# A two-layer decoder step on one core: norms and query weights taken ahead, fewer level-two candidates, sample sums as wide rows

## The chip, the cores and the metric

The kernel runs on one core of one Trainium2 chip. The metric is the time of one execution in device microseconds. A lower time is better. All times below are microseconds unless they are marked ns.

## What is computed

One inference step of a decoder trunk with two layers: 512 prompt tokens and 8 sample tokens (520 in all), width 1024, all in 32-bit floats. Layer 0 mixes by mLSTM and RWKV-7, layer 1 by HGRN2. Behind each stands a PEER mixer, which holds most of the time. The reference, cut:

```python
for l in range(DEPTH):                                   # DEPTH = 2
    sh1, sc1, g1, sh2, sc2, g2 = split(silu(c) @ ada_w[l] + ada_b[l], 6)
    h = _rmsnorm(x, norm_mix_g[l]) * (1 + sc1) + sh1
    out = _even_mixer(h, ...) if l % 2 == 0 else _odd_mixer(h, ...)
    x = x + g1 * out
    h = _rmsnorm(x, norm_ffn_g[l]) * (1 + sc2) + sh2
    x = x + g2 * _peer(h, peer_w_q[l], peer_keys[l], peer_u[l], peer_v[l])
y = _rmsnorm(x, norm_final_g)

def _peer(h, w_q, keys, u_tab, v_tab):                   # 8 heads, 2 x 128 keys, 16384 experts
    q = (h @ w_q).reshape(T, 8, 2, 128)
    s = einsum('thcd,hckd->thck', q, keys)
    s_top, i_top = lax.top_k(s, 16)
    cand = s_top[:, :, 0, :, None] + s_top[:, :, 1, None, :]
    best, pos = lax.top_k(cand.reshape(T, 8, 256), 16)   # 16 experts of each head
    gate = jax.nn.softmax(best)
    act = jax.nn.gelu(einsum('thkd,td->thk', u_tab[experts], h))
    return einsum('thk,thkd->td', gate * act, v_tab[experts])
```

## The kernel before

Columns of x and h are tokens, and the 1024 features lie in 8 pieces (DT) of 128 partitions. A product of 32-bit data is made as three matmuls of high and low parts in fp32r (x high by w high, x high by w low, x low by w high): each operand is cast to its high part on ACT, and DVE or POOL subtracts that for the low part. The program is a row of stages, each a block with one instruction list for each engine. An engine enters the next block when all have left the last.

`mix_norm` at the head of a layer squares x on ACT, adds the squares in pairs on DVE, sums over partitions with ones-matmuls (L731), takes root and reciprocal, and scales x. `split_stage` is the projection behind it (L301 with the high parts of the tokens, L309 with the low parts); both output projections (`residual_projection`) use it too, and add the gated result to x on DVE.

`peer_start` (L2266) makes the second norm and the queries: 8 squares (L2391), 8 ones-matmuls (L2351), root (L2396), reciprocal by token halves (L2454), x times it in four steps of 4 pieces (L2463), the high parts of the tokens on ACT (L2402). The query weights come in blocks of 256 columns by DMA (`load_w`, L2284), become high (`high_q`, L2255) and low (`low_q`, L2261) parts, and the first matmuls with them are L2367, those with the low parts of the tokens L2344. The 16 transposes of the keys are L2357.

`peer_hidden` (L2551) goes over all 16384 experts in 128 units. The prompt tokens are handled densely: in a unit PE makes the hidden values of 128 experts for 512 tokens (24 matmuls, L2841), with rows of u that DVE turns (L2224), ACT casts (L2232) and POOL subtracts (L2237). Between these, DVE finds each token's experts (`routing`): for each of the four tiles of 128 tokens it adds 16 by 16 level-one scores to 256 candidates a head (L2667), finds the best 16 of each head by `top16_rows` (MAX L2520 and L2531, FIND_INDEX L2525 and L2536, MATCH_REPLACE L2526), turns positions into two numbers (L2671 to L2675), and picks the keys (L2682 to L2696). PE turns the picks (L2850), behind unit `pick_unit` less LEAD = 2, and then makes the gates in groups of four tokens (the quads, L2868). The generator's `yield` numbers are costs: a planner of the kernel spends 4.4 us of them a unit, and so fixes in which unit each step stands on every engine. For the 8 sample tokens only the chosen rows of u and v are gathered. Their output sums are L2859: for each sample 8 matmuls, each with 128x128 of the gathered rows as stationary operand and one column of gates times hidden values as moving operand, 32 matmuls for each batch of four samples.

`peer_outputs` (L3042) is the second pass over the 128 units, with the gates and the rows of v (24 matmuls a unit, L3098), and in layer 0 at its end x + gate times result in 8 steps on DVE (L3088). `final_output` (L3562) does the same step after layer 1 (L3628), transposes x (L3599), squares and sums on ACT (L3612), and scales by tile of tokens (L3641).

## Time and profile before

| | us |
|---|---|
| median of 3 runs | 4648.28 |
| lowest and highest run | 4644.43, 4651.64 |
| the profiled execution | 4645.92 |
| its span in the profile | 4644.2 |
| PE busy | 4383.8 (94%) |
| DVE busy | 2930.1 (63%) |
| ACT busy | 1989.4 (43%) |
| POOL busy | 1353.6 (29%) |
| mean granted TensorE clock | 0.968 of full speed |

Busy is the time in which an engine executes; what an engine issues or waits for is not in it. The profiled execution lies 1.7 us outside its own span, and 2.4 us under the median. In the time line rows a row is a run of like instructions with its start, its duration and, in brackets, the idle time of the engine ahead of it and what ended that. A 32-bit matmul is recorded twice, an fp32r one once.

### The profile page before, as it was taken

Reading aid. Unit: us, or ns where it says so; the run is one execution under the profiler, and the core shown is the slowest. Engines: PE = TensorE matmul, PEld = TensorE weight load, DVE = VectorE, ACT = ScalarE, POOL = GpSimd, SP = SyncE. Lnnn points to the kernel's source line nnn. Section 1 sums busy time; section 2 is a strip of 40 time slices with the busy share of each in tenths; the row PEclk is TensorE's granted clock in tenths of the full one; section 3 lists DMA queues with packets and bytes.
Section 4 is the critical chain, followed back from the end, with each engine's and each line's share of the span. In section 5 each row is a group of like instructions: output and inputs, shape, how many; then the busy total and the mean of one; then the engine's idle time right before and its main releaser. Section 6 shows DMA issues by size and latency. Waiting matters only on the chain. (4 is left out here: it accounts for less than half of the span.)

```text
span 4644.2 us, 66922 instructions
## 1 busy us (share of the span) xinstructions
PE 4383.8 (94%) x26123; PEld 3645.2 (78%) x26123; DVE 2930.1 (63%) x4667; ACT 1989.4 (43%) x4172; POOL 1353.6 (29%) x609
## 2 busy tenths in 40 slices
PE   8996888999999999999989977999999999999998
PEld 6964678878888878888869756887878887888887
DVE  3265655899745536666663378589964553666665
ACT  3221223278767832222222223327875783222222
POOL 0000001333433344444430000133343334444443
PEclk9997999999999999999999988999998999999999
DMA  4241225256866665555533321425686666555553
GB/s 165 79 139 50 77 67 114 64 152 177 248 179 179 180 210 182 199 199 184 196 107 100 128 81 42 102 72 157 172 236 176 175 179 212 185 201 195 185 200 111
DMA packets 553451, 703.26 MB, mean 151 GB/s; under 512 B 54361, under 2 KB 457426, under 8 KB 532658
## 3 DMA queue, kind: packets, MB, share of 16 engines
q1 hardware_dynamic: 545540, 681.40, 47.0%
q0 software_dynamic: 4608, 16.78, 1.1%
q8 instruction: 208, 3.41, 0.3%
q10 hardware_dynamic: 2990, 0.82, 0.1%
q14 instruction: 105, 0.86, 0.1%
HBM read 549.44 MB, written 145.01 MB: 150 GB/s over the span
## 5 line engine op out<-in xcount | busy, mean ns | idle before, releaser
L2841 PE MATMUL ps<-h_parts,u_parts 128*128 128x512 f32 x6144 | 1490.0, 399 | 14.9 <-POOL u_parts L2237 7.1
L2841 PEld LDWEIGHTS ps<-h_parts,u_parts 128*128 128x128 f32 x6144 | 1156.0, 191 | 281.6 <-POOL u_parts L2237 17.5
L3098 PE MATMUL ps<-w_parts,v_parts 128*128 128x512 f32 x4080 | 938.8, 389 | 0.0
L2237 POOL TENSOR_TENSOR u_parts<-u_turned,u_parts 128x1024 fp32r<-128x1024 f32 x256 | 620.5, 2424 | 1021.2 <-ACT u_parts L2232 1021.1
L3098 PEld LDWEIGHTS ps<-w_parts,v_parts 128*128 128x128 f32 x4080 | 765.9, 188 | 158.9
L2224 DVE STREAM_TRANSPOSE u_turned<-u_rows 128x1024 f32<-128x1024 f32 x256 | 317.9, 1242 | 308.6 <-POOL u_parts L2237 195.6
L3098 PE MATMUL ps<-first_w,first_v 128*128 128x512 f32 x2064 | 485.3, 391 | 6.7 <-PEq L2765 6.7
L3098 PEld LDWEIGHTS ps<-first_w,first_v 128*128 128x128 f32 x2064 | 389.6, 189 | 88.8 <-issue 7.5
L2750 ACT ACTIVATE onehots<-onehots,choice 128x128 fp32r<-128x128 f32 x1024 | 328.2, 399 | 3.6 <-DVE onehots L2723 3.4
L2754 ACT ACTIVATE onehots<-onehots,choice 128x128 fp32r<-128x128 f32 x1024 | 325.6, 393 | 0.0
L2261 POOL TENSOR_TENSOR u_parts<-w_q_first,u_parts 128x1024 fp32r<-128x1024 f32 x20 | 47.9, 2397 | 910.8 <-ACT u_parts L2255 910.8
L2232 ACT CAST u_parts<-u_turned 128x1024 fp32r<-128x1024 f32 x256 | 270.7, 1057 | 94.2 <-DVE u_turned L2224 94.2
L3038 DVE TENSOR_TENSOR w_parts<-w_rows,w_parts 128x512 fp32r<-128x512 f32 x86 | 211.2, 2456 | 157.9 <-ACT w_parts L3033 157.9
L2745 ACT ACTIVATE hidden<-ps 128x512 f32<-128x512 f32 x256 | 152.0, 594 | 367.7 <-PE ps L2841 338.6
L2723 DVE TENSOR_TENSOR onehots<-ps,choice 128x1024 fp32r<-128x1024 f32 x256 | 306.4, 1210 | 0.1
L3038 DVE TENSOR_TENSOR w_parts<-first_rows,w_parts 128x512 fp32r<-128x512 f32 x84 | 202.6, 2412 | 160.5 <-ACT w_parts L3033 160.5
L3017 POOL TENSOR_TENSOR v_parts<-u_rows,v_parts 128x1024 fp32r<-128x1024 f32 x86 | 207.4, 2413 | 272.6 <-ACT v_parts L3011 272.6
L3017 POOL TENSOR_TENSOR first_v<-u_rows,first_v 128x1024 fp32r<-128x1024 f32 x86 | 206.7, 2404 | 262.3 <-ACT first_v L3011 262.3
L2738 DVE TENSOR_TENSOR h<-ps,h 128x512 f32<-128x512 f32 x256 | 169.1, 674 | 178.6 <-ACT h L2762 175.4
L3017 POOL TENSOR_TENSOR v_parts<-v_rows,v_parts 128x1024 fp32r<-128x1024 f32 x84 | 200.7, 2389 | 253.2 <-ACT v_parts L3011 253.2
L3011 ACT CAST v_parts<-u_rows 128x1024 fp32r<-128x1024 f32 x86 | 90.4, 1051 | 322.0 <-PE ps L3098 316.9
L3011 ACT CAST first_v<-u_rows 128x1024 fp32r<-128x1024 f32 x86 | 90.4, 1051 | 317.7 <-PE ps L3098 317.7
(577 smaller groups left out, 5995.2 us busy)
## 6 DMA issues: line engine op xcount, KB each, us to landing
u_rows<-in_peer_u_dram SPq DMA_DIRECT2D x1024, 128.0 KB
u_rows<-in_peer_v_dram SPq DMA_DIRECT2D x86, 1024.0 KB, 4.9
hidden_tiles<-hidden SPq DMA_DIRECT2D x256, 256.0 KB
gate_matrices<-h SPq DMA_DIRECT2D x64, 1024.0 KB, 7.3
gates<-gate_matrices SPq DMA_DIRECT2D x32, 2048.0 KB, 8.2
u_turned<-hidden_tiles SPq DMA_DIRECT2D x256, 256.0 KB, 3.4
arena<-in_ada_w_dram SPq DMA_DIRECT2D x48, 1024.0 KB, 5.4
v_rows<-in_peer_v_dram SPq DMA_DIRECT2D x42, 1024.0 KB, 4.9
```

Source lines behind the costliest of these rows:

```text
L2224: s.nc.vector.transpose(q.uT[:, n % 2].rearrange("p k (b e) -> p k b e", b=4), q.u[:, slot, :, n % TJ, :].rearrange("p b (k i) -> p k b i" ...
L2232: s.nc.scalar.copy(q.uTs[:, (n + 1) % 3, 0], q.uT[:, n % 2]).then_inc(q.u_high.sem, 1)
L2237: s.nc.gpsimd.tensor_tensor(q.uTs[:, (n + 1) % 3, 1], q.uT[:, n % 2], q.uTs[:, (n + 1) % 3, 0].bitcast(F32), ALU.subtract).then_inc(q.u_re ...
L2723: nc.vector.tensor_tensor(q.hot[:, k % GATE_RING, 0:3:2], iota.unsqueeze(1).unsqueeze(1).to_broadcast(eight), q.choice[:, 0:2, 4 * k:4 * k ...
L2738: nc.vector.tensor_tensor(place, quad_parts(k)[:, :, P:2 * P].rearrange("p t (a j) -> p t a j", j=GJ), place, ALU.add).then_inc(q.gates_ad ...
L2750: ins = nc.scalar.mul(q.hot[:, k % GATE_RING, 1, i, :], f32(q.hot[:, k % GATE_RING, 2, i, :]), q.choice[:, 2, 4 * k + i:4 * k + i + 1])
L2754: ins = nc.scalar.mul(rest, f32(rest), q.choice[:, 3, 4 * k + i:4 * k + i + 1])
L2841: ins = mm(ps[:, n % 2, :], q.uTs[:, (n + 1) % 3, wp, k, :], q.hs[:, xp, k, 0:T], start=k == 0 and (wp, xp) == (0, 0), stop=k == DT - 1 an ...
L3011: s.nc.scalar.copy(q.vs[n % 3][:, 0], q.v[slot][:, n % TJ, :]).then_inc(q.v_high.sem, 1)
L3017: s.nc.gpsimd.tensor_tensor(q.vs[n % 3][:, 1], q.v[slot][:, n % TJ, :], q.vs[n % 3][:, 0].bitcast(F32), ALU.subtract).then_inc(q.v_ready.s ...
L3038: s.nc.vector.tensor_tensor(q.ws[n % 3][:, 1], q.w[n % 2], q.ws[n % 3][:, 0].bitcast(F32), ALU.subtract).then_inc(q.w_ready.sem, 1)
L3098: ins = nc.tensor.matmul(ps[:, o, :], q.vs[n % 3][:, vp, o * P:(o + 1) * P], q.ws[n % 3][:, wp], start=n == 0 and (vp, wp) == (0, 0), stop ...
```

## The change

- **Layer 1's first norm.** `mix_norm` is left out for layer 1. In the last unit of layer 0's `peer_outputs` PE signals after each of its 8 output pieces, DVE adds the gated result for each, ACT squares it, POOL (pieces 0, 2, 4) and DVE (6) add the squares in pairs. In the projection (`split_stage` with `scaled_here`) follow the ones-matmuls by token halves, root, reciprocal and scaling by halves, and the first unit's matmuls by halves. The low part of its first weights is made on POOL, and the loads of its first three weight blocks are issued in this block.
- **The second norm.** In both output projections ACT squares the pieces 0 to 6 and DVE adds them to one sum, a group behind the drains. `peer_start` squares the last one and needs 4 ones-matmuls in place of 8. The first block of query weights is loaded into space of its own during the output projection (4 DMAs, ahead of those of the modulation and of x on SP's queue). `low_q` of the first two pieces is made on POOL, not DVE. The 16 transposes of the keys stand behind the second query group's high parts, not ahead of the first. `high_q` of the third piece stands ahead of the copies of the keys.
- **Candidates.** Of 16 by 16 sums the 16 best can only be among the first 4 rows (16 wide) and, in the 12 rows behind, the first 4 columns: 64 + 48 = 112 a head. They are made in two steps, searched as 112 columns, and the position is decoded in 11 small steps (before 6). The planner gets lower costs, and PE's picks stand one unit nearer to DVE's.
- **Sample sums.** For each sample 2 matmuls of 32-bit data with 8 columns as stationary operand (zero but for the sample's own, so that 8 samples add up) and 512 columns of the gathered rows as moving operand, into partitions 0 to 7 and 32 to 39 of one PSUM bank; DVE copies them out, 8 transposes (L2961 of the kernel after) turn them.
- **The end.** The gated result of layer 1 is added as in layer 0; in `final_output` the mean of the next tile is made ahead of the scaling of this one.

```diff
+            if scaled_here:
+                for j in range(2):
+                    for k in range(0, DT, 2):
+                        ins = nc.tensor.matmul(sums[:, j, 0:HALF[j + 1] - HALF[j]], s.ones[:], h[:, k, part(j)],
+                                               start=k == 0, stop=k == DT - 2)
+                    ins.then_inc(s.sum_ready.sem, 1)
+                by_high_halves()
...
+                    dve.wait_ge(s.root_ready.sem, s.root_ready.at(2 + j))
+                    link(v.reciprocal(s.rstd[:, part(j)], s.rstd[:, part(j)]))
+                    if j == 1:
+                        link(v.tensor_tensor(side, s.x[:, :, T:N], s.rstd[:, T:N].unsqueeze(1).to_broadcast([P, DT, B]), ALU.mult))
+                        link(v.tensor_tensor(side, side, s.modA[:, :, 1:NB], ALU.mult))
+                        link(v.tensor_tensor(side, side, shift[:, :, 1:NB], ALU.add))
+                        link(v.tensor_copy(hh[:, 0, :, T:N], side))
+                        v.tensor_tensor(hh[:, 1, :, T:N], side, hh[:, 0, :, T:N].bitcast(F32), ALU.subtract).then_inc(s.h_side.sem, 1)
+                    four = s.rstd[:, tokens[j]].unsqueeze(1).to_broadcast([P, 4, 256])
+                    for k in (0, 4):
+                        v.tensor_tensor(h[:, k:k + 4, tokens[j]], s.x[:, k:k + 4, tokens[j]], four, ALU.mult).then_inc(
+                            s.xn_ready.sem, 1)
...
+    def squares(act, i):
+        if i:
+            k = i - 1
+            act.wait_ge(s.dve_drained.sem, s.dve_drained.at(k + 1))
+            if k >= 3:
+                act.wait_ge(s.sq_paired.sem, s.sq_paired.at(k - 2))
+            nc.scalar.activation(s.squares[:, k % 2] if k else s.rstd[:], s.x[:, k, :], ACT.Square).then_inc(s.sq_ready.sem, 1)
+
+    def summed(dve, i):
+        if i >= 2:
+            k = i - 1
+            dve.wait_ge(s.sq_ready.sem, s.sq_ready.at(k + 1))
+            if k >= 2:
+                dve.wait_ge(s.sq_paired.sem, s.sq_paired.at(k - 1))
+            nc.vector.tensor_tensor(s.rstd[:], s.rstd[:], s.squares[:, k % 2], ALU.add).then_inc(s.sq_paired.sem, 1)
+
     def moved(sp):
+        load_w(s, s.peer, sp, layer, 0)
...
-            load_w(0)
+            load_w(s, q, sp, layer, 1)
             for head in range(NH):
                 sp.dma_start(q.keys[:, 2 * head:2 * head + 2, :],
                              s.io["peer_keys"][layer, head].rearrange("c k d -> k c d")).then_inc(q.keys_loaded.sem, 16)
-            for b in range(1, WQ):
-                load_w(b)
+            for b in range(2, WQ):
+                load_w(s, q, sp, layer, b)
...
-            for k in range(0, DT, 2):
-                pe.wait_ge(s.sq_paired.sem, s.sq_paired.at(k // 2 + 1))
-                for j, part in enumerate((left, right)):
-                    ins = mm(ps[:, j, 0:widths[j]], s.ones[:], q.sq[:, k, part], start=k == 0, stop=k == DT - 2)
-                    if k == DT - 2:
-                        ins.then_inc(s.sum_ready.sem, 1)
-            pe.wait_ge(q.keys_loaded.sem, q.keys_loaded.at(16 * NH))
-            for g in range(4):
-                for i in range(4):
-                    ins = nc.tensor.transpose(ps[:, 4 + g, i * P:(i + 1) * P], q.keys[:, 4 * g + i, :], s.ident[:])
-                ins.then_inc(q.keys_made.sem, 1)
+            pe.wait_ge(s.sq_paired.sem, s.sq_paired.at(DT - 2))
+            for j, part in enumerate((left, right)):
+                mm(ps[:, j, 0:widths[j]], s.ones[:], s.rstd[:, part], start=True, stop=False)
+            pe.wait_ge(s.sq_ready.sem, s.sq_ready.at(DT))
+            for j, part in enumerate((left, right)):
+                mm(ps[:, j, 0:widths[j]], s.ones[:], q.sq[:, part], start=False, stop=True).then_inc(s.sum_ready.sem, 1)
...
+            pe.wait_ge(q.keys_loaded.sem, q.keys_loaded.at(16 * NH))
+            for g in range(4):
+                for i in range(4):
+                    ins = nc.tensor.transpose(ps[:, 4 + g, i * P:(i + 1) * P], q.keys[:, 4 * g + i, :], s.ident[:])
+                ins.then_inc(q.keys_made.sem, 1)
...
-            link(v.tensor_tensor(eq4(q.cand[:]), top[:, 0].unsqueeze(3).to_broadcast(four),
-                                 top[:, 1].unsqueeze(2).to_broadcast(four), ALU.add))
-            yield 2.3
-            yield from top16_rows(s, dve, q.gate[:], q.pos, q.cand[:], q.work[:], NH)
+            for first, last, at, width in ((0, 4, 0, TOPK), (4, TOPK, 4 * TOPK, 4)):
+                shape = [P, NH, last - first, width]
+                ins = v.tensor_tensor(q.cand[:, :, at:at + (last - first) * width].rearrange("p h (k a) -> p h k a", a=width),
+                                      top[:, 0, :, first:last].unsqueeze(3).to_broadcast(shape),
+                                      top[:, 1, :, 0:width].unsqueeze(2).to_broadcast(shape), ALU.add)
+            link(ins)
+            yield 1.3
+            yield from top16_rows(s, dve, q.gate[:], q.pos, q.cand[:, :, 0:LIKELY], q.work[:], NH)
+            place, start, row = (q.work[:, i, 0:HK].rearrange("p (h k) -> p h k", h=NH) for i in range(3))
+            v.tensor_copy(q.best[:], q.gate[:, :, 0:1])
+            v.tensor_copy(place, q.pos)
             link(v.tensor_scalar(q.posa, q.pos, 4, None, ALU.logical_shift_right))
-            link(v.tensor_scalar(q.pos, q.pos, 15, None, ALU.bitwise_and))
-            v.tensor_copy(q.best[:], q.gate[:, :, 0:1])
+            link(v.tensor_scalar(q.pos, q.pos, 2, None, ALU.logical_shift_right))
             v.tensor_copy(q.ab[:, 0], q.posa)
-            link(v.tensor_copy(q.ab[:, 1], q.pos))
+            link(v.tensor_copy(row, q.pos))
+            link(v.scalar_tensor_tensor(q.ab[:, 0], row, -12.0, q.ab[:, 0], ALU.add, ALU.max))
+            link(v.tensor_scalar(start, q.ab[:, 0], 4.0, 48.0, ALU.mult, ALU.add))
+            link(v.scalar_tensor_tensor(start, q.ab[:, 0], 16.0, start, ALU.mult, ALU.min))
+            link(v.tensor_tensor(q.ab[:, 1], place, start, ALU.subtract))
             v.tensor_tensor(q.gate[:], q.gate[:], q.best[:].to_broadcast([P, NH, TOPK]),
                             ALU.subtract).then_inc(q.shifted.sem, 1)
             exp_unit[t] = now[0]
-            yield 1.5
+            yield 2.6
...
-            v.tensor_tensor(r.hidm[:], r.hid[:], r.gateT[:], ALU.mult).then_inc(q.s_weighted.sem, 1)
+            v.tensor_tensor(r.hidm[:][:, 0:B * B:B + 1], r.hid[:], r.gateT[:], ALU.mult).then_inc(q.s_weighted.sem, 1)
             unit["sums"] = now[0]
             while now[0] < unit["sums"] + 9:
                 yield 0.0
             dve.wait_ge(q.s_summed.sem, q.s_summed.at(B))
-            unit["summed"] = now[0]
-            link(v.tensor_tensor(s.tmp8[:], sums, mod_part(s, 5)[:, :, 1:NB], ALU.mult))
+            v.tensor_copy(flat[:, 0:512], ps[0:B, 6, :])
+            v.tensor_copy(flat[:, 512:D], ps[32:32 + B, 6, :]).then_inc(q.s_flat.sem, 1)
...
-                    if pick_unit[t] == n + LEAD or (n == 0 and pick_unit[t] < LEAD):
+                    if pick_unit[t] == n + 1 or (n == 0 and pick_unit[t] < 1):
...
-                        for k in range(DT):
-                            ins = mm(sums[:, k, t:t + 1], rows_of[:, t % 4, k * P:(k + 1) * P], r.hidm[:, t:t + 1],
-                                     start=True, stop=True)
+                        for half in range(2):
+                            ins = mm(ps[32 * half:32 * half + B, 6, :], r.hidm[:, t * B:(t + 1) * B],
+                                     rows_of[:, t % 4, half * 512:(half + 1) * 512], start=t == 0, stop=t == B - 1)
                         ins.then_inc(q.s_summed.sem, 1)
+                if n == unit["flat"]:
+                    pe.wait_ge(q.s_flat.sem, q.s_flat.at(1))
+                    for k in range(DT):
+                        ins = nc.tensor.transpose(ps[:, 6, k * B:(k + 1) * B], flat[:, k * P:(k + 1) * P], s.ident[0:B, 0:B])
+                    ins.then_inc(q.s_columns.sem, 1)
...
+                for k in range(DT):
+                    act.wait_ge(s.xn_ready.sem, s.xn_ready.at(k + 1))
+                    nc.scalar.activation(s.h[:, k, :], s.x[:, k, :], ACT.Square).then_inc(s.sq_ready.sem, 1)
 
         @block.gpsimd
         def _(pool):
             for n in range(1, NK):
                 low_v(s, q, pool, n)
+            if layer < LAYERS - 1:
+                for k in range(0, DT - 2, 2):
+                    pool.wait_ge(s.sq_ready.sem, s.sq_ready.at(k + 2))
+                    nc.gpsimd.tensor_tensor(s.h[:, k, :], s.h[:, k, :], s.h[:, k + 1, :], ALU.add)
...
+            gate = mod_part(s, 5)
+            for k in range(DT):
+                dve.wait_ge(q.out_sum.sem, q.out_sum.at(NK + k))
+                nc.vector.scalar_tensor_tensor(s.x[:, k, 0:T], ps[:, k, :], gate[:, k, 0:1], s.x[:, k, 0:T],
+                                               ALU.mult, ALU.add).then_inc(s.xn_ready.sem, 1)
             if layer < LAYERS - 1:
-                gate = mod_part(s, 5)
-                dve.wait_ge(q.out_sum.sem, q.out_sum.at(NK))
-                for k in range(DT):
-                    nc.vector.scalar_tensor_tensor(s.x[:, k, 0:T], ps[:, k, :], gate[:, k, 0:1], s.x[:, k, 0:T],
-                                                   ALU.mult, ALU.add)
+                k = DT - 2
+                dve.wait_ge(s.sq_ready.sem, s.sq_ready.at(DT))
+                nc.vector.tensor_tensor(s.h[:, k, :], s.h[:, k, :], s.h[:, k + 1, :], ALU.add)
...
-            for k in range(DT):
-                v.scalar_tensor_tensor(x[:, k, 0:T], ps[:, k, :], gate[:, k, 0:1], x[:, k, 0:T],
-                                       ALU.mult, ALU.add).then_inc(updated.sem, 1)
+
+            def mean(t):
+                n = rows(t)
+                dve.wait_ge(squared.sem, squared.at(TT + t + 1 if t < TT else 2 * TT + 2))
+                link(v.tensor_tensor(f.scale[0:n, t:t + 1], f.sums[0:n, t, 0:1], f.sums[0:n, t, 1:2], ALU.add))
+                v.tensor_scalar(f.scale[0:n, t:t + 1], f.scale[0:n, t:t + 1], 1.0 / D, EPS, ALU.mult, ALU.add).then_inc(summed.sem, 1)
+
+            mean(0)
```

On DVE, the first tile's position decode, before (posa, pos and ab are positions, gate the scores, best the highest; gates is the working buffer):

```order
L2671 TENSOR_SCALAR posa<-pos 128x128
L2672 TENSOR_SCALAR pos<-pos 128x128
L2673 COPY best<-gate 128x8
L2674 CAST ab<-posa 128x128
L2675 CAST ab<-pos 128x128
L2676 TENSOR_TENSOR gate<-gate,best 128x128
L2682 TENSOR_TENSOR gates<-ab,ps 128x2048
L2224 STREAM_TRANSPOSE u_turned<-u_rows 128x1024
L2686 TENSOR_TENSOR gates<-gates,ps 128x2048
```

and after:

```order
L2762 COPY best<-gate 128x8
L2763 CAST gates<-pos 128x128
L2764 TENSOR_SCALAR posa<-pos 128x128
L2765 TENSOR_SCALAR pos<-pos 128x128
L2766 CAST ab<-posa 128x128
L2767 CAST gates<-pos 128x128
L2768 SCALAR_TENSOR_TENSOR ab<-gates,ab 128x128
L2769 TENSOR_SCALAR gates<-ab 128x128
L2770 SCALAR_TENSOR_TENSOR gates<-ab,gates 128x128
L2771 TENSOR_TENSOR ab<-gates 128x128
L2772 TENSOR_TENSOR gate<-gate,best 128x128
L2778 TENSOR_TENSOR gates<-ab,ps 128x2048
```

The two shifts stay, five small steps are new, and behind them come the same wide steps of the pick.

On PE, unit by unit around the first batch of sample sums, before (s_hidm is gates times hidden values, gates the gathered rows):

```order
L2841 MATMUL ps<-h_parts,u_parts 128x512 x24
L2859 MATMUL ps<-s_hidm,gates 128x1 x32
L2868 MATMUL ps<-onehots 128x256 x4
L2841 MATMUL ps<-h_parts,u_parts 128x512 x24
L2868 MATMUL ps<-onehots 128x256 x4
```

and after:

```order
L2937 MATMUL ps<-h_parts,u_parts 128x512 x24
L2955 MATMUL ps<-gates,s_hidm 8x512 x8
L2969 MATMUL ps<-onehots 128x256 x4
L2937 MATMUL ps<-h_parts,u_parts 128x512 x24
L2969 MATMUL ps<-onehots 128x256 x4
L2937 MATMUL ps<-h_parts,u_parts 128x512 x24
```

32 matmuls with one moving column became 8 with 512; the 8 transposes stand four units behind the second batch.

On PE, from the second norm to the queries of a PEER mixer, before (gates holds the squares, u_turned the keys, u_parts the query weights):

```order
L2351 MATMUL ps<-gates,ones 128x256
L2351 MATMUL ps<-gates,ones 128x264
L2357 MATMUL ps<-ident,u_turned 128x128 x16
L2367 MATMUL ps<-h_parts,u_parts 128x256 x16
L2367 MATMUL ps<-h_parts,u_parts 128x264 x16
L2336 MATMUL ps<-h_parts,u_parts 128x256
L2336 MATMUL ps<-h_parts,u_parts 128x264
```

and after:

```order
L2434 MATMUL ps<-rstd,ones 128x256
L2434 MATMUL ps<-rstd,ones 128x264
L2437 MATMUL ps<-gates,ones 128x256
L2437 MATMUL ps<-gates,ones 128x264
L2446 MATMUL ps<-h_parts,u_parts 128x256 x16
L2446 MATMUL ps<-h_parts,u_parts 128x264 x16
L2420 MATMUL ps<-h_parts,u_parts 128x256
L2420 MATMUL ps<-h_parts,u_parts 128x264
```

The transposes of the keys no longer stand ahead of the first query matmuls, and four ones-matmuls are left, two of them on the sum made in rstd.

## Rows read from the trace of the kernel before

**Rows 1.** Page, part 5: op, names, shapes, count | busy, mean ns | idle before

```profile
L2841 PE MATMUL ps<-h_parts,u_parts 128*128 128x512 f32 x6144 | 1490.0, 399 | 14.9 <-POOL u_parts L2237 7.1
```

**Rows 2.** Time line, layer 1's norm and projection: start, us, engine, op [idle before, releaser]

```profile
2414.81 5.36 DVE L3088 SCALAR_TENSOR_TENSOR x<-ps,mod,x 128x512 f32<-128x512 f32 x8 [12.25 <-PE ps L3098]
...
2439.81 9.67 PE L301 MATMUL ps<-odd_h_parts,odd_w_in_parts 128*128 128x256 f32 x64 [11.57 <-DVE odd_h_parts L373]
...
2449.32 4.02 PE L309 MATMUL ps<-odd_h_parts,odd_w_in_parts 128*128 128x256 f32 x32
```

**Rows 3.** Time line, start of layer 0's PEER mixer

```profile
745.85 4.32 ACT L2391 ACTIVATE gates<-x 128x520 f32<-128x520 f32 x8 [11.95 <-PEq L278]
...
746.15 2.63 SPq L2290 DMA_DIRECT2D h<-x  x4
...
756.35 1.04 ACT L2255 CAST u_parts<-w_q_first 128x1024 fp32r<-128x1024 f32 x1 [6.18 <-DMA w_q_first<-in_peer_w_q_dram]
...
758.57 1.75 DVE L2454 RECIPROCAL rstd<-rstd 128x256 f32<-128x256 f32 x1
759.38 3.28 PEld L2357 LDWEIGHTS ps<-ident,u_turned 128*128 128x128 f32 x16 [6.82 <-DMA u_turned<-in_peer_keys_dram]
...
760.35 2.36 DVE L2463 TENSOR_TENSOR h<-h,rstd 128x1024 f32<-128x1024 f32 x2
```

**Rows 4.** Time line, the same place in layer 1

```profile
2953.10 1.04 ACT L2255 CAST u_parts<-w_q_first 128x1024 fp32r<-128x1024 f32 x1 [5.50 <-DMA w_q_first<-in_peer_w_q_dram]
```

**Rows 5.** Time line of PE, first units of layer 0's hidden pass

```profile
886.77 12.96 PE L2841 MATMUL ps<-h_parts,u_parts 128*128 128x512 f32 x48 [3.26 <-PEq L2276]
...
943.59 0.90 PE L2850 MATMUL ps<-ident,picked 128*128 128x128 f32 x3 [5.83 <-DVE picked L2696]
944.15 19.03 PE L2841 MATMUL ps<-h_parts,u_parts 128*128 128x512 f32 x72
```

**Rows 6.** DVE by line and form, 887 to 943.6; the last is L2671 over both layers

```profile
L2525 DVE FIND_INDEX8 pos<-gate,gates 128x8 uint32<-128x256 f32 x8 | 3.4, 419 | 0.0
...
L2667 DVE TENSOR_TENSOR gates<-gates 128x2048 f32<-128x2048 f32 x1 | 3.3, 3273 | 0.0
...
L2525 DVE FIND_INDEX8 gates<-gates 128x8 uint32<-128x128 f32 x8 | 2.3, 285 | 0.0
...
L2671 DVE TENSOR_SCALAR posa<-pos x8: 226/574/2055, 921.8 to 3323.2; 128x128 uint32<-128x128 uint32 x8
```

**Rows 7.** Time line of PE around the sample sums of layer 0

```profile
1318.64 8.66 PE L2859 MATMUL ps<-s_hidm,gates 128*128 128x1 f32 x64
...
1328.16 7.01 PE L2841 MATMUL ps<-h_parts,u_parts 128*128 128x512 f32 x24
...
1335.48 5.75 PE L2841 MATMUL ps<-h_parts,u_parts 128*128 128x512 f32 x24
...
1365.79 11.19 PE L2859 MATMUL ps<-s_hidm,gates 128*128 128x1 f32 x64
...
1377.84 7.71 PE L2841 MATMUL ps<-h_parts,u_parts 128*128 128x512 f32 x24
```

**Rows 8.** Windows: from:to us, busy (count) of PE, PEld, DVE, ACT, POOL, granted clock, DMA share, GB/s

```profile
1365.79:1376.84 11.05, 11.05 (x66) 11.05 (x64) 1.25 (x1) 0.60 (x1) 0.00 (x0) 0.62 0.42 120
...
944.00:950.00 6.00, 6.00 (x20) 4.75 (x19) 5.97 (x10) 1.05 (x1) 1.36 (x1) 0.61 0.37 111
```

**Rows 9.** Time line of PE in layer 0's mixer: two halves of PSUM, then one

```profile
474.74 4.54 PE L1618 MATMUL ps<-arena,sel 128*64 128x256 f32 x40
479.21 3.62 PE L627 MATMUL ps<-arena,sc 128*9 128x256 f32 x16
```

**Rows 10.** Time line, the final output

```profile
4624.93 5.29 PE L3599 MATMUL ps<-ident,x 128*128 128x128 f32 x32 [3.11 <-DVE x L3628]
...
4632.10 1.41 DVE L3641 SCALAR_TENSOR_TENSOR arena<-ps,arena 128x512 f32<-128x512 f32 x2
...
4634.23 1.41 DVE L3641 SCALAR_TENSOR_TENSOR arena<-ps,arena 128x512 f32<-128x512 f32 x2
```

244 lines of the change are left out of this document (150 added, 94 removed).

## The prediction, made before the changed kernel was run

> **What bounds the kernel now.** I read the page first: PE is busy for 94% of the span, and one line, the hidden values, holds 1490 us of it with only 14.9 us of idle time ahead [rows 1]. That work stays as it is. What a change can give lies in the few places where PE waits for another engine, and in PE work that goes away. So I read the time line stage by stage where PE's rows have a bracket, and the granted clock of the windows around them. There are five such places, and the change touches each.
>
> **A, the norm of layer 1.** PE's last output matmul ends at about 2414.8, when DVE begins the 8 gated additions [rows 2]. The first projection matmul starts at 2439.81, and the low parts of the tokens let L309 start at 2449.32 [rows 2], 9.5 later. After the change 7 of the 8 additions (5.36 / 8 = 0.67 each) lie beside matmuls. Behind 2414.8 come the last addition (0.7), one square (4.32 / 8 = 0.54 [rows 3]), one addition of squares (about 0.7, priced like the gated one), a block change (0.5, my assumption), four ones-matmuls of the left half (0.45 each, [rows 9], see D: 1.8), its root (0.4, assumed) and reciprocal (1.75 [rows 3]): 2421.2. DVE then makes two scaling steps (2.36 [rows 3]), the right half's reciprocal (1.75), five sample steps (some 1.3) and two more scaling steps (2.36): 2429.0. From there it has the same low parts to make as before, 9.5 with one low part of weights. The second kind of matmuls thus starts at 2438.5 to 2439 instead of 2449.32: **-10.5**. The high parts by halves end before that and cost nothing, nor do the weights, whose loads are issued first in the block. If ACT, which has the roots, a weight cast and 16 half-wide high parts in a row, gets late, 8; if the clock that PE keeps is better, 13.
>
> **B, the second norm, in both layers.** The block begins at 745.85, the first scaling step at 760.35, 14.5 later [rows 3]. In between stand 8 squares and their sums, and ACT, which waits 6.18 for query weights before it casts them ahead of the root [rows 3]. After the change: one square (0.54), the cast (1.04, its data there before the block), the table load and root (about 1.7, the time from the end of that cast's row to the start of the reciprocal is 1.2, and a table load may come to it), the reciprocal (1.75): about 5.1. The fourth quarter of x, which that step also needs, is issued by 748.8 [rows 3], 2.9 after the begin; with a landing of some 2 it stands just beside this, so 5.1 it is: 9.4 saved. But the 16 key transposes, which now lie in the wait for keys [rows 3], move onto PE's path; 1.9, about half of their 3.3 there, since PE in part waits anyway for the tokens' low parts. Layer 0: -7.5. In layer 1 the weights' wait is 5.50 [rows 4], 0.7 less: -6.9. Squares and sums in the output projection (7 of 0.54 on ACT, 6 of about 0.7 on DVE) lie beside its matmuls, where ACT sits idle for 11.95 before the block [rows 3]; without that cover they would cost up to 4 a layer. The weights' four DMAs delay 44 others on SP by 2 to 3, none of which is waited for at once. The low parts moved to POOL take 2.4 instead of 1.2, and POOL is idle there. Sum **-14.4**, with 10 and 18 as ends.
>
> **C, the first picks of each layer.** PE stands 5.83 for the picks at 943.59, after eight units [rows 5]. DVE is what it waits for, and DVE is busy throughout: its chain is searching and picking with the turns of u between. A FIND_INDEX of 256 columns is 419 ns, of 128 columns 285 [rows 6], so 1.05 ns a column. With 112 columns each of the 5 x 8 scans loses 144 columns: 40 x 0.15 = 6.0. The candidates fall from 2048 to 896 elements; 3.27 [rows 6] becomes 1.1 to 1.4 in two steps, so 1.9 less. Five more small steps of 226 ns (the least of the shift, [rows 6]) add 1.2. One turn of u (1.24) that stood ahead of the picks now stands behind them. Sum: the picks come 7.9 earlier, at about 935.7. PE's first eight units are busy for 12.96 (two, [rows 5]) and 6 x 5.75 [rows 7], 47.5 from 886.77, so they can end at 934.2; they ended at 943.59 - 5.83 = 937.8, with 3.5 of short waits for u, which shrink as DVE is relieved. So PE gains about 8, not 5.83: both the wait and part of the short ones. Then the clock: three units behind the wait take 19.03 [rows 5], at a granted 0.61 in their first 6 us [rows 8], against 3 x 5.6 = 16.8 undisturbed, so 2.2 more if there is no wait to fall cold in. 10.3 a layer, and layer 1 has the same pattern: **-20.6**. If the short waits stay and PE still stands for a moment, only 6 a layer; 12.5 if all goes.
>
> **D, the sample sums, in both layers.** The two batches of 32 matmuls take 8.66 and 11.19 [rows 7], with a clock of 0.62 in the second [rows 8], and the units behind them 7.01 and 7.71 instead of 5.75 [rows 7]; with the quads next to them (1.1 more, estimated) that is 19.6 + 3.2 + 1.1 = 24.0 a layer. The new operation is not in the trace. The nearest rows: 20 matmuls of 256 columns, whose results go by turns to two halves of PSUM's partitions, follow each other in 4.47, 0.22 each; 8 into one place take 3.62, 0.45 each [rows 9]. A matmul of 512 columns should then cost 0.9, and a pair, if its two run side by side, 0.9 together. 8 pairs: 7.2, or 14.4 one after another. The 8 transposes behind cost 0.17 each (5.29 / 32 [rows 10]), 1.3, their wait hidden by the distance of four units. I take 8.5, since L1618 shows the side-by-side case at nearly this shape. And the clock: a stream of wide columns keeps it, for L627's rows with 9 columns of weights run at 0.45 for 256 columns, so nothing is added behind. 2 x (24.0 - 8.5) = **-31.0**. Ends: -35 with layer 1's sums slower than layer 0's, -17 with the pairs in series.
>
> Here a page has a say. The Trainium skill, "TensorE: Matmul & The Clock Gate", Part 3, says that a weight load overlaps matmuls in flight only when the row group differs. The two halves of a pair use all rows and differ in columns alone, so by it they would go one after another, and the sum of D would be about -17. The trace speaks against it: 0.22 against 0.45 [rows 9].
>
> **E, the end.** Transposes stand 3.11 for the first gated additions [rows 10]; with the additions beside the last matmuls some 1.2 stay, -1.9. The scaled tiles follow each other at 2.13 (4632.10, 4634.23), 1.41 of it in the two multiplications [rows 10]; with the next mean made early, 0.5 less for three tiles, -1.5. **-3.4**, with 2 and 5 as ends.
>
> **Sum.** -10.5 - 14.4 - 20.6 - 31.0 - 3.4 = -79.9. Against the profiled execution's 4645.9 that gives **4566.0**. The median of the runs is 2.4 above that execution, so 4568 would do as well.
>
> **The rivals.**
> - *The pairs in series.* The sums cost 15.7 a layer, not 8.5: 14.4 more, 4580. For it speaks that no row has 8-column weights over 512 columns of 32-bit data; against it [rows 9].
> - *PE finds the next wait in C.* The first picks come early, but the units ahead keep their waits for u, since DVE is full there anyway: 4.3 less a layer, 4575.
> - *The clock gives more.* PE's waits in A and B fall short enough that the units behind them start warm, 2 to 3 at each of four places: 4556.
> - *Small gains hidden.* ACT is late in A and the fourth quarter of x or the keys in B: both ends, 2.5 + 4.4 less, with C's lower end 4582.
> - *DVE steps held up by POOL, slower than before.* One and the same shift took 226 ns at best and 2055 at worst [rows 6]: 1.83 more. POOL makes low parts beside it in every unit. The decode has 11 such steps for each of 8 tiles. If each were held up like that, and DVE's lateness reached PE in every tile, 11 x 8 x 1.83 = 161 would be added: 4727. It decides from (79.9 + 9.3) / 88 = 1.0 us a step. Against it: the median of those eight is 574, and steps that follow at once on a held-up one find POOL done. The Trainium skill, "SBUF — State Buffer", Who interferes with whom, says that DVE and GpSimd hold a shared pair of ports for a whole instruction and the other blocks; the 2055 of one step in a row of short ones agrees, and by it one step a tile at most would pay for each instruction of POOL.
>
> **How the numbers follow.** Chances: forecast 0.50, pairs in series 0.15, next wait 0.14, clock 0.08, hidden gains 0.08, held up by POOL 0.03 for slower (and 0.02 for about no change, where half of it comes true). The forecast's own range is 4558 to 4574. With the series, the next wait and the clock it becomes **4553 to 4589**, which leaves out less than 2 in 10. Slower or faster by 0.2% (9.3 us) is about what a measurement of this kernel can tell from no change. Faster 0.95, same 0.02, slower 0.03.
>
> **What would show it.** In the profile after: the projection's second kind of matmuls at 24 us behind the last output matmul (before 34.5); the first scaling step at 5 us in both PEER blocks; the picks' matmuls without a bracket above 1 and the three units behind them under 17.5; the sample sums below 4.5 a batch and the units behind them at 5.75. It is wrong if the batches take 7 or more (series), if PE's bracket at the picks is 3 or more, or if DVE's small steps have a mean above 0.5 us.

## The result

| | before | after |
|---|---|---|
| median of 3 runs | 4648.28 | 4608.21 |
| lowest, highest | 4644.43, 4651.64 | 4607.22, 4618.05 |
| the profiled execution | 4645.92 | 4608.21 |
| its span | 4644.2 | 4606.5 |

The ratio after to before is 0.9919, with a 95% interval of 0.9904 to 0.9934. The change makes the kernel 0.8% faster, 40 us by the medians and 38 by the profiled executions. The forecast was 80, and 4608 lies outside 4553 to 4589. The page of the kernel after:

```profile
span 4606.5 us, 66608 instructions
...
PE 4347.4 (94%) x25931; PEld 3591.5 (78%) x25931; DVE 2899.5 (63%) x4715; ACT 1994.0 (43%) x4180; POOL 1367.3 (30%) x617
...
L2937 PE MATMUL ps<-h_parts,u_parts 128*128 128x512 f32 x6144 | 1479.8, 397 | 12.9 <-PEq L2368 6.5
```

The line of the hidden values that stands in [rows 1] is L2937 now. PE's busy time fell by 36 and PE is still at 94%.

To find the place of a loss, I set the same points of PE's list beside each other in both traces: the first or last matmul of each stage. Each column is the time between two such points. The two input projections are not in the table; they differ by 0.8 together.

| stage | before | after | forecast | found |
|---|---|---|---|---|
| layer 0's mixer (projection to output projection; unchanged) | 461.2 | 464.4 | 0 | +3.2 |
| B: end of its output projection to first hidden unit | 142.8 | 137.2 | -7.5 | -5.6 |
| C and D: hidden pass, layer 0 | 826.1 | 817.8 | -25.8 | -8.3 |
| output pass, layer 0 | 701.5 | 701.5 | 0 | 0 |
| A: its end to the projection's second kind of matmuls | 34.9 | 29.9 | -10.5 | -5.0 |
| layer 1's mixer (unchanged) | 270.7 | 273.3 | 0 | +2.6 |
| B in layer 1 | 142.7 | 137.2 | -6.9 | -5.5 |
| C and D: hidden pass, layer 1 | 835.7 | 821.0 | -25.8 | -14.7 |
| output pass, layer 1 | 701.6 | 702.5 | 0 | +0.9 |
| E: the end | 22.8 | 18.3 | -3.4 | -4.5 |

The two hidden passes hold 28.6 of the 42 that are missing from the 80 forecast (79.9 less 37.7 between the two spans). The stretch in which the wait of [rows 5] stood, on PE (start, us, engine, line, op, count, then idle time ahead and its releaser):

```profile
922.38 11.68 PE L2937 MATMUL ps<-h_parts,u_parts 128*128 128x512 f32 x48 [1.97 <-POOL u_parts L2321]
934.12 0.55 PE L2946 MATMUL ps<-ident,picked 128*128 128x128 f32 x3
934.43 5.83 PE L2937 MATMUL ps<-h_parts,u_parts 128*128 128x512 f32 x24
...
946.18 0.69 PE L2969 MATMUL ps<-onehots 128*128 128x256 f32 x4
948.48 0.74 PE L2969 MATMUL ps<-onehots 128*128 128x256 f32 x4 [1.60 <-ACT onehots L2850]
949.05 5.83 PE L2937 MATMUL ps<-h_parts,u_parts 128*128 128x512 f32 x24
961.39 1.20 PE L2969 MATMUL ps<-onehots 128*128 128x256 f32 x4 [6.51 <-DVE h L2834]
962.38 7.22 PE L2937 MATMUL ps<-h_parts,u_parts 128*128 128x512 f32 x24
```

The picks come without any wait, 50.5 behind the first hidden matmul instead of 56.8. But three units on stands a new wait of 6.51, on DVE's addition of gates (L2834), and the unit behind it takes 7.22 instead of 5.75. Layer 1 has the same 6.51 at the same unit. What DVE did then shows in its own time line:

```profile
950.40 1.23 DVE L2308 STREAM_TRANSPOSE u_turned<-u_rows 128x1024 f32<-128x1024 f32 x1
951.55 1.19 DVE L2819 TENSOR_TENSOR onehots<-ps,choice 128x1024 fp32r<-128x1024 f32 x1
...
954.74 2.28 DVE L2762 COPY best<-gate 128x8 f32<-128x8 f32 x1
956.94 0.21 DVE L2763 CAST gates<-pos 128x128 f32<-128x128 uint32 x1
...
959.22 0.29 DVE L2772 TENSOR_TENSOR gate<-gate,best 128x128 f32<-128x128 f32 x1
959.43 1.24 DVE L2308 STREAM_TRANSPOSE u_turned<-u_rows 128x1024 f32<-128x1024 f32 x1
960.59 1.25 DVE L2834 TENSOR_TENSOR h<-ps,h 128x512 f32<-128x512 f32 x2
```

From one turn of u (950.40) to the next (959.43) DVE has one comparison, 8 FIND_INDEX steps and the whole decode of the next tile: 9.0, where PE needs about 6.1 for a unit. The gates' addition, first in the next unit, is what PE waits for. The windows between the turns of u say it in numbers (from:to us, busy and count of PE, PEld, DVE, ACT and POOL, granted clock, DMA share, GB/s):

```profile
940.27:945.62 5.35, 5.12 (x22) 4.19 (x23) 5.28 (x15) 3.04 (x8) 2.58 (x2) 1.00 0.51 151
945.62:950.40 4.78, 3.18 (x18) 2.47 (x17) 4.75 (x19) 4.78 (x15) 0.48 (x1) 1.00 0.13 51
950.40:959.43 9.03, 4.48 (x20) 3.27 (x18) 8.76 (x31) 7.00 (x20) 4.28 (x2) 0.96 0.61 177
959.43:965.20 5.77, 3.81 (x11) 3.26 (x12) 5.74 (x7) 2.58 (x6) 0.97 (x1) 0.50 0.47 136
```

DVE is full in each, as it was before. Three theories came out of this. **Theory 1**: the planner's lower costs are at fault. It spends a fixed 4.4 of cost in each unit, so cheaper steps do not make a unit lighter; they only bring the next tile's steps forward. PE is held by DVE's full units, so it gains nothing. **Theory 2**: the eleven-step decode itself, one step of it held up for 2 us, is at fault wherever it stands. **Theory 3**: the loss lies elsewhere or is scatter.

### The profile page after: what moved, and what is told of

It is laid out like the page before. It is cut to its first block and busy times, and to the rows that moved or that the text cites. A ratio compares the mean times of both kernels' runs of the same rounds, so it can differ in the third digit from the quotient of the medians.

```text
span 4606.5 us, 66608 instructions
## 1 busy us (share of the span) xinstructions
PE 4347.4 (94%) x25931; PEld 3591.5 (78%) x25931; DVE 2899.5 (63%) x4715; ACT 1994.0 (43%) x4180; POOL 1367.3 (30%) x617
## 3 DMA queue, kind: packets, MB, share of 16 engines
q0 software_dynamic: 4608, 16.78, 1.1%
## 5 line engine op out<-in xcount | busy, mean ns | idle before, releaser
L2937 PE MATMUL ps<-h_parts,u_parts 128*128 128x512 f32 x6144 | 1479.8, 397 | 12.9 <-PEq L2368 6.5
L2937 PEld LDWEIGHTS ps<-h_parts,u_parts 128*128 128x128 f32 x6144 | 1147.8, 190 | 277.0 <-POOL u_parts L2321 17.7
L2316 ACT CAST u_parts<-u_turned 128x1024 fp32r<-128x1024 f32 x256 | 270.6, 1057 | 90.1 <-DVE u_turned L2308 90.1
L2834 DVE TENSOR_TENSOR h<-ps,h 128x512 f32<-128x512 f32 x256 | 169.4, 675 | 178.5 <-ACT h L2858 174.7
L2345 POOL TENSOR_TENSOR u_parts<-w_q_ahead,u_parts 128x1024 fp32r<-128x1024 f32 x8 | 18.9, 2374 | 814.0 <-ACT u_parts L2339 814.0
```

Of the source, the lines that this page charges most:

```text
L2316: s.nc.scalar.copy(q.uTs[:, (n + 1) % 3, 0], q.uT[:, n % 2]).then_inc(q.u_high.sem, 1)
L2834: nc.vector.tensor_tensor(place, quad_parts(k)[:, :, P:2 * P].rearrange("p t (a j) -> p t a j", j=GJ), place, ALU.add).then_inc(q.gates_ad ...
L2937: ins = mm(ps[:, n % 2, :], q.uTs[:, (n + 1) % 3, wp, k, :], q.hs[:, xp, k, 0:T], start=k == 0 and (wp, xp) == (0, 0), stop=k == DT - 1 an ...
```

## The experiments

Each kernel is compared with the kernel before on the same chip; several runs each unless it says one.

### The candidates undone

```diff
-            yield 1.3
-            yield from top16_rows(s, dve, q.gate[:], q.pos, q.cand[:, :, 0:LIKELY], q.work[:], NH)
+            yield 2.3
+            yield from top16_rows(s, dve, q.gate[:], q.pos, q.cand[:], q.work[:], NH)
...
-            yield 2.6
+            yield 1.5
...
-                    if pick_unit[t] == n + 1 or (n == 0 and pick_unit[t] < 1):
+                    if pick_unit[t] == n + LEAD or (n == 0 and pick_unit[t] < LEAD):
```

> The changed kernel with its candidate part alone undone: 256 candidates a head, the six-step decode, the old costs of the planner and the picks two units behind on PE. In the trace of the changed kernel the hidden pass loses 9.8 us (layer 0) and 9.1 us (layer 1) against before from its first unit to unit 55. Theory 1 (the denser plan of DVE's work is the loser) and theory 2 (the longer decode is the loser) both expect about 19 us less than the changed kernel, 4589. Theory 3 (those losses come from something else in the change, or are no more than scatter of this program) expects 4603 to 4613.

Measured: 4596.75 (4591.07 to 4605.45), before 4645.1 beside it, ratio 0.9908 (0.9886 to 0.9929). The ratio alone does not part it from the changed kernel's 0.9919. The hidden passes are 812.2 and 810.0 instead of 817.8 and 821.0: undoing the part gains 5.6 and 11.0 there, 17 in all, against the 19 that theories 1 and 2 gave. Against theory 3 speaks a finer reading. In both layers this kernel begins each of the first 50 hidden units within 0.6 of the time at which the kernel before begins it, counted from the first unit, and unit 50 itself within 0.1. The changed kernel begins unit 50 later, by 13.3 in layer 0 and 16.4 in layer 1. So the loss up to there comes with the candidate part, and not from elsewhere in the change.

### The candidates alone, on the kernel before

The same hunks the other way round, with nothing else of the change.

> The kernel before with the candidate part of the change alone, with its new costs. Theory 1 (the denser plan loses more than the cheaper scans give): slower than before by the 12 us by which undoing it made the changed kernel faster, up to the 19 us that the trace of the changed kernel loses in the two hidden passes up to unit 55: 4656 to 4664. The prediction's term C had it 20.6 us faster: 4624.

Measured: 4659.55 (4652.34 to 4667.37), before 4637.9 beside it, ratio 1.0048 (1.0031 to 1.0066): slower than before by 0.5%. The part that the prediction had at 20.6 us of gain is a loss. In its profile the hidden passes are 834.1 and 835.2, 8.0 more and 0.5 less than in the profile of the kernel before; up to unit 50 the loss is alike in both layers, 10.6 and 11.4. The same waits stand in its trace, 1.61 and 5.05 at the gates:

```profile
940.14 0.55 PE L2861 MATMUL ps<-ident,picked 128*128 128x128 f32 x3
...
954.52 0.73 PE L2879 MATMUL ps<-onehots 128*128 128x256 f32 x4 [1.61 <-ACT onehots L2765]
...
967.50 1.19 PE L2879 MATMUL ps<-onehots 128*128 128x256 f32 x4 [5.05 <-DVE h L2749]
```

### The new steps with the old costs

```diff
-            yield 1.3
-            yield from top16_rows(s, dve, q.gate[:], q.pos, q.cand[:, :, 0:LIKELY], q.work[:], NH)
+            yield 2.3
+            yield from top16_rows(s, dve, q.gate[:], q.pos, q.cand[:, :, 0:LIKELY], q.work[:], NH, scan=0.406)
...
-            yield 2.6
+            yield 1.5
```

> The changed kernel with the same 112 candidates and eleven-step decode, but with the costs the planner had for 256 candidates (2.3, 0.406 a scan, 1.5 for the decode), so that each tile's steps stand in the units in which they stood before. Theory 1 (the cheaper costs pack the routing into fewer units, so DVE is as full in each unit as before and only done earlier): each unit gets lighter, no wait of 6.5 us at the gates, 4572 to 4585, faster than the kernel with the candidate part undone. Theory 2 (the eleven steps themselves, with one held up by POOL for 2 us, overfill the unit they stand in): 4600 to 4610, near the changed kernel.

Measured: 4579.14 (4578.35 to 4584.19), ratio 0.987 (0.9852 to 0.9887). DVE's work is that of the changed kernel to the last step; three numbers of the plan are other, and the time falls by 29 us against it by the medians, by 23 by the ratios. The hidden passes are 804.2 and 804.8, 29.8 less together. So theory 2 falls, and that the lower costs are at fault stands. On PE:

```profile
933.24 0.49 PE L2946 MATMUL ps<-ident,picked 128*128 128x128 f32 x3
933.48 11.40 PE L2937 MATMUL ps<-h_parts,u_parts 128*128 128x512 f32 x48
...
952.41 0.71 PE L2969 MATMUL ps<-onehots 128*128 128x256 f32 x4 [0.57 <-DVE h L2834]
...
979.41 1.14 PE L2969 MATMUL ps<-onehots 128*128 128x256 f32 x4 [2.07 <-DVE h L2834]
```

0.57 and 2.07 are left of the waits at the gates. This kernel begins the ninth hidden unit, which in the kernel before stands behind the picks, 10.3 earlier than before in both layers: the size that term C had. At unit 27, counted from 0, it is still 10.6 ahead.

Which sum went into the unit of 9.0 can be worked out from the costs. The planner deals a further step as long as anything of the 4.4 is left. The comparison costs 1.25 and the 8 FIND_INDEX steps 2 x (4 x 0.262 + 0.3) = 2.7, so 0.45 was left, and the whole decode went in as well. With the old costs, 0.406 a scan, half of those steps stand one unit earlier, as this kernel's trace shows.

### The picks two units behind again

```diff
-                    if pick_unit[t] == n + 1 or (n == 0 and pick_unit[t] < 1):
+                    if pick_unit[t] == n + LEAD or (n == 0 and pick_unit[t] < LEAD):
```

> The kernel with the old costs (4579), and PE's transposes of the picks two units behind DVE's numbering again (before: pick unit less 2), not one. If the closer place is what let PE pass the first picks without a wait, PE stands there 1 to 4 us in each layer and falls to a lower clock: 4582 to 4590. If lighter DVE units did it alone: 4577 to 4581.

Measured: 4576.86 (4573.46 to 4578.45), ratio 0.9855 (0.9836 to 0.9874), not to be told from 0.987. PE does wait 4.15 for the first picks in each layer, as the first expectation had it, and yet the hidden passes are 805.4 and 802.1. The wait stands in place of short ones behind it: 0.57 and 2.07 at the gates are gone, and by unit 27 PE is as far as without the wait (10.0 ahead of before, for 10.6). In these units DVE's pace counts, and where PE stands still for it does not.

### A planner that carries what a unit overspends

```diff
-                credit = UNIT_WORK
+                credit = UNIT_WORK - debt
...
+                debt = 0.0
                 while credit > 0:
                     spent = next(work, None)
-                    if spent is None:
+                    if not spent:
                         break
-                    credit -= spent if spent > 0 else UNIT_WORK
+                    credit -= spent
+                    debt = max(0.0, -credit)
...
-            yield 2.6
+            yield 5.0
```

> The changed kernel with a planner that carries a unit's overspending into the next one, and a cost of 5.0 for the decode (its eleven steps with one hold take 4.7 us in the trace), 1.3 and 0.262 for the rest. The picks come in units 10, 23, 38 and 53 in place of 8, 17, 27 and 37. Theory 1 (what counts is that no unit holds more DVE work than PE's 6.1 us): the waits at the gates go, apart from those for memory; but the first picks come two units later than in the changed kernel, which costs nothing while PE is not held: 4568 to 4578. Rival (the first picks' wait on PE comes back, as in the kernel before, or the long decode still overfills its own unit): 4580 to 4600.

Measured: 4568.75 (4566.54 to 4573.09), ratio 0.9839 (0.982 to 0.9859). Hidden passes 798.1 and 796.4, 20 and 25 less than in the changed kernel with the same steps on every engine. The ratio's interval overlaps that of the old costs; the hidden passes, 6 and 8 shorter, part the two. The carrying and the decode's new cost came in together, and neither was tried alone. 130 us from the first hidden unit on, in the kernel before, the changed one and this one (columns as in the windows above):

```profile
886.77:1016.77 130.00, 117.50 (x504) 93.59 (x505) 128.56 (x275) 69.48 (x151) 47.27 (x19) 0.96 0.46 135
```

```profile
883.59:1013.59 130.00, 118.40 (x510) 94.20 (x511) 124.84 (x326) 73.75 (x167) 45.63 (x19) 0.96 0.46 135
```

```profile
885.77:1015.77 130.00, 130.00 (x577) 105.82 (x578) 126.12 (x295) 81.91 (x182) 53.61 (x22) 0.99 0.51 153
```

DVE is busy for 125 to 129 in all three. PE is busy for 117.5, 118.4 and 130.0, and so gets through more units in the same time. What sets PE's time is how many units DVE's work is spread over. The first picks are turned at 943.17 in this kernel, 57.4 behind the first unit and thus as late as before, but behind ten units, not eight, and without any wait.

### The sample sums undone

```diff
-                        for half in range(2):
-                            ins = mm(ps[32 * half:32 * half + B, 6, :], r.hidm[:, t * B:(t + 1) * B],
-                                     rows_of[:, t % 4, half * 512:(half + 1) * 512], start=t == 0, stop=t == B - 1)
+                        for k in range(DT):
+                            ins = mm(sums[:, k, t:t + 1], rows_of[:, t % 4, k * P:(k + 1) * P], r.hidm[:, t:t + 1],
+                                     start=True, stop=True)
```

> The changed kernel with the sample sums alone as before: 64 matmuls with one moving column a layer, no transposes. The prediction's term D gives 31 us more than the changed kernel, and its trace (two batches of 3.6 us, 0.66 us for the transposes, no slower unit behind) 32: 4640. If the pairs' gain is partly given back elsewhere (the gathers and stores around it), 4625 to 4635.

Measured: 4647.21 (4641.51 to 4649.08), ratio 1.0005 (0.9993 to 1.0018), no difference from before. Without its part D the change gives nothing that can be measured. Its hidden passes are 833.4 and 836.8 against 817.8 and 821.0, 15.6 and 15.8 more: 31.4, where the prediction had 31.0. The medians say 40, for layer 0's mixer (467.1) and the projection ahead of it (245.4 for 242.8) of this run were slow too.

### Both halves of a pair in one place

```diff
-            v.tensor_copy(flat[:, 512:D], ps[32:32 + B, 6, :]).then_inc(q.s_flat.sem, 1)
+            v.tensor_copy(flat[:, 512:D], ps[0:B, 6, :]).then_inc(q.s_flat.sem, 1)
...
-                            ins = mm(ps[32 * half:32 * half + B, 6, :], r.hidm[:, t * B:(t + 1) * B],
-                                     rows_of[:, t % 4, half * 512:(half + 1) * 512], start=t == 0, stop=t == B - 1)
+                            ins = mm(ps[0:B, 6, :], r.hidm[:, t * B:(t + 1) * B],
+                                     rows_of[:, t % 4, half * 512:(half + 1) * 512], start=(t, half) == (0, 0), stop=(t, half) == (B - 1, 1))
```

All 16 matmuls of a layer add up in one place here.

> The changed kernel with both halves of each sample's sums written to the same eight partitions, so that no pair can run side by side; the two halves are added up together, which leaves out that each stands for its own columns of the output. If pairs run side by side in the changed kernel (3.54 us for four of them), a batch takes 6.9 to 7.2 us here, and the whole 14 us more, as the prediction's rival had it. If they already run one after another, a batch stays at 3.5.

Measured, one run: 4626.26. The batch in the changed kernel and here:

```profile
1287.99 3.61 PE L2955 MATMUL ps<-gates,s_hidm 128*8 128x512 f32 x16
```

```profile
1288.74 7.03 PE L2955 MATMUL ps<-gates,s_hidm 128*8 128x512 f32 x16
```

3.61 against 7.03: four pairs side by side in 3.5, 0.89 a pair, or one after another, 0.87 a matmul. By the four batches this kernel takes 13.7 more than the changed one, and by the hidden passes (824.3 and 828.1) 13.6. Whether the pairs need other partitions, or only another place to add up in, these two kernels do not tell apart.

### Low parts back on DVE

```diff
             v.memset(s.small[:, 0:1], EPS).then_inc(s.root_ready.sem, 1)
+            low_q(s, q, dve, 0)
...
-                if scaled_here:
-                    proj.low(nc.gpsimd, 0)
                 pool_first(pool)
...
+                    if j == 0:
+                        proj.low(v, 0)
```

(and the second query piece likewise, behind the scaling steps of the right half.)

> The changed kernel with the low parts of the first query weights (two in each layer) and of the first weights of layer 1's projection made on DVE again, not on POOL; that of the projection stands behind the first two scaling steps. Theory P (a low part on POOL holds up DVE's scaling step beside it: 4.11 to 4.35 us for two steps instead of 2.36 in three places): the three places get 1.0 to 1.8 each, 3 to 5 in all: 4603 to 4605. Rival (the two scaling steps are slow for another reason, and DVE now has 1.2 more in each place): 4610 to 4612.

Measured: 4609.19 (4601.63 to 4615.92), ratio 0.9926 (0.9907 to 0.9944): by its time nothing can be told. By its stages, B is 134.7 and 134.8 instead of 137.2 twice, and A 29.2 instead of 29.9. The scaling step in the changed kernel beside POOL's low part, and here without it:

```profile
749.84 4.65 POOL L2345 TENSOR_TENSOR u_parts<-w_q_ahead,u_parts 128x1024 fp32r<-128x1024 f32 x2 [288.63 <-ACT u_parts L2339]
...
752.59 4.11 DVE L2544 TENSOR_TENSOR h<-h,rstd 128x1024 f32<-128x1024 f32 x2 [0.48 <-DMA h<-x]
```

```profile
754.23 2.36 DVE L2545 TENSOR_TENSOR h<-h,rstd 128x1024 f32<-128x1024 f32 x2
```

POOL's second subtraction ends at 754.49, and ACT, which waits for DVE's first scaling step, starts at 755.60: the step ran its own 1.2 only behind POOL's. By the stages the gain is 5.6; the profiled execution lost it again in the unchanged mixers (467.2 and 277.3, against 464.4 and 273.3) and in a hidden pass 4.8 longer.

### The old costs, low parts on DVE, and the root's table ahead

```diff
                 act.wait_ge(s.root_ready.sem, s.root_ready.at(1))
+                nc.scalar.activation(s.small[:, 2:3], s.small[:, 0:1], ACT.Sqrt, bias=s.small[:, 0:1], scale=1.0)
```

> The kernel with the old costs (4579) and two more edits: the low parts of the first weights back on DVE, and a root of one small column on ACT ahead of its wait in layer 1's projection, so that the table load of 1.28 us lies in ACT's idle time. In the trace with the low parts on DVE the stretch from the output projection's end to the first hidden unit was 134.6 and 134.8 us, against 137.3 and 137.2 in the changed kernel, but its total did not show it. Theory P (POOL's low part holds up the scaling steps, and the table load stands on the path): 2.7 + 2.4 + 0.7 + 1.3 = 7 less, 4572. Rival (these moments are taken up again by the next wait): 4577 to 4581.

Measured: 4571.85 (4559.31 to 4588.53), ratio 0.9857 (0.983 to 0.9883). The median is where theory P had it, but the interval holds the rival as well. The stages are clear: B 134.7 and 134.8, A 27.0, 2.2 less than with the low parts alone. The ones-matmuls ahead of the root take the same 5.4 in both.

### All that helped

The carrying planner, low parts on DVE and the early root in one kernel.

> The changed kernel with the carrying planner and true costs, the low parts of the first weights on DVE and the root of a small column ahead of the wait. By stages of the profiles so far: the hidden passes of the carrying planner (798.1 and 796.4), the stretches between projection and hidden pass with low parts on DVE (134.7 and 134.8, before 137.2), 27.0 behind the output pass (28.5 in the carrying kernel): 2.5 + 2.4 + 1.5 = 6 less than 4568.75, so 4562. If the unchanged mixers come out slow, as they differ by 10 us from run to run, up to 4572.

Measured: 4552.7 (4546.77 to 4558.48), before 4637.9 beside it, ratio 0.9811 (0.9798 to 0.9825). Hidden passes 793.9 and 797.4, B 134.7 and 134.8, A 25.9. That is 1.9% faster than before and 1.1% than the changed kernel, by the ratios. The expectation, 4562, was 9 too high; the kernel before stood 6.5 lower beside this run than beside the carrying one, and by the stages it is 4.8 shorter than the carrying kernel in B, 2.6 in A and 3.2 in the hidden passes, where 6 was expected in all.

## Why the prediction was wrong

**The step that failed** is in term C: the picks' wait was priced as if nothing else of the plan moved with it. "So PE gains about 8, not 5.83", and no word on the costs of the `yield` lines, although the text on the change names them. The scans did get cheaper, the picks did come earlier (the 7.9 of the prediction is 6.3 by the distance from the first unit, for PE stands 2.95 for u ahead of them), and PE passed them without a bracket. But the planner had been given the lower costs, and spent what was saved on the next tile. A decode that cost the plan 2.6 and DVE 4.7 fell into one unit with 8 scans and a comparison, and the wait came back three units later as 6.51. Of the signs that the prediction named, this is the one that failed: the three units behind the picks end 20.5 behind the first one's start (934.43 to 954.88), not under 17.5. The prediction had a rival of this kind, "PE finds the next wait in C", but for another reason, that waits for u would stay, at 4.3 less a layer and a chance of 0.14. The loss was much larger. The forecast was -10.3 a layer; against the kernel without it the part costs 5.6 and 11.0. So 16 and 21 went missing, 37 of the 42. (The table of stages shows only 29, because the kernel before loses 5.67 and 2.75 to waits for memory in its second hidden pass, and the kernel without the part only 3.09.) With the old costs, the same steps gave the 10.3 up to the ninth unit.

The wait of 6.51 is not the whole loss. This table follows PE through layer 0: when a hidden unit begins, counted from the first one, less the same time in the kernel before. Units are counted from 0. Up to unit 50, layer 1 agrees within 0.4, but for the changed kernel's 16.4 and the 11.4 of the candidates alone.

| unit | part undone | changed | part alone | old costs | picks two behind | carrying |
|---|---|---|---|---|---|---|
| 8 | 0.0 | -6.5 | -6.5 | -10.3 | -5.4 | -11.1 |
| 12 | 0.0 | +2.7 | +3.2 | -11.2 | -6.6 | -13.8 |
| 27 | 0.0 | 0.0 | +0.1 | -10.6 | -10.0 | -13.5 |
| 40 | 0.0 | +6.1 | +6.3 | -8.6 | -10.0 | -11.4 |
| 50 | 0.0 | +13.3 | +10.6 | -6.9 | -8.6 | -12.4 |

By unit 27 the changed kernel has nothing left of its lead, and at unit 50 it is 13.3 behind the kernel before. At the end of that stretch PE waits 6.13 in layer 0 and 8.67 in layer 1, some 335 behind the first unit, where DVE has stood 8.89 and 9.85 for rows of u from memory. The kernel before waits 2.76 and 5.67 there, the one with the old costs 2.12 and 4.11, the carrying one no more than 1.9 at any place of the pass.

Nor is it the fullest single unit that holds PE. The kernel with the old costs has a unit of 9.32 on DVE as well (busy for 9.01, between the turns of u of units 6 and 7), and PE has no wait above 0.3 from unit 3 until behind the picks. What decides is how much of DVE's work stands ahead of a given unit. From the turn of u of unit 3 to that of unit 40, in the kernel before, the changed one, with the old costs, and carrying (columns as in the windows above):

```profile
902.15:1130.00 227.85, 215.63 (x980) 175.25 (x980) 225.93 (x427) 160.54 (x387) 88.32 (x36) 0.99 0.54 157
```

```profile
898.56:1134.65 236.09, 222.72 (x1014) 180.51 (x1013) 226.68 (x486) 169.93 (x409) 89.51 (x37) 0.99 0.56 161
```

```profile
894.79:1116.58 221.79, 217.19 (x991) 177.26 (x990) 206.18 (x451) 161.78 (x392) 88.28 (x37) 0.99 0.58 163
```

```profile
897.98:1113.09 215.11, 213.25 (x974) 174.55 (x973) 195.06 (x370) 155.75 (x375) 87.35 (x36) 0.99 0.57 167
```

For the same 37 units DVE is busy for 225.9, 226.7, 206.2 and 195.1. The cheaper steps with lower costs left it as much to do ahead of unit 40 as before, in more steps. A unit then takes DVE 6.2, 6.4, 6.0 and 5.8, where PE with its gates needs about 6.1.

**A** was half of what was forecast, -5.0 for -10.5. The rows of the changed kernel show which terms were mis-sized:

```profile
2405.78 5.43 PE L340 MATMUL ps<-h,ones 128*128 128x256 f32 x16 [2.50 <-PEq L3155]
...
2409.38 1.28 ACT L373 ACT_TABLE_LOAD   x1 [4.63 <-PE ps L340]
2410.67 1.06 ACT L373 ACTIVATE rstd<-ps,small 128x256 f32<-128x256 f32 x2
2411.24 1.75 DVE L427 RECIPROCAL rstd<-rstd 128x256 f32<-128x256 f32 x1 [5.19 <-ACT rstd L373]
...
2413.03 4.35 DVE L436 TENSOR_TENSOR h<-x,rstd 128x1024 f32<-128x1024 f32 x2
```

The ones-matmuls of the left half let ACT go 3.6 behind their start, for 1.8 in the sum, priced from rows at full clock. The granted clock was 0.53 in these 3.6. In the carrying kernel, with the same steps there, it was 1.00, ACT went 2.04 behind their start, and A took 28.5 in place of 29.9:

```profile
2388.23 3.75 PE L340 MATMUL ps<-h,ones 128*128 128x256 f32 x16 [2.50 <-PEq L3157]
...
2390.27 1.28 ACT L373 ACT_TABLE_LOAD   x1 [3.08 <-PE ps L340]
```

So the price was right for the full clock; which clock would be granted there was not weighed. The root's table load, 1.28, was not in A's sum at all; it stands behind ACT's wait. The two scaling steps take 4.35 for 2.36, beside POOL. Together 1.8 + 1.3 + 2.0 = 5.1 of the 5.5 missing, and the last two were undone: 29.9 became 27.0 at the same low clock.

**B** was -5.6 and -5.5 for -7.5 and -6.9. The scaling step did begin 4.4 behind the block's start, as forecast (5.1), but took 1.75 longer. "POOL is idle there" was true and not the point: the first scaling step beside POOL's work took 2.98, for 1.22 without it. With the low parts on DVE B is -8.1 and -7.9.

**D** was right, and so was its mechanism: 15.6 and 15.8 by the kernel without it, for 15.5 a layer. 3.54 a batch for 3.6 forecast, 0.66 for the transposes for 1.3, granted clock 1.00 in the batch and behind it, where [rows 8] had 0.62:

```profile
1287.99:1291.53 3.54, 3.54 (x17) 0.68 (x16) 0.00 (x0) 0.60 (x1) 0.00 (x0) 1.00 0.22 78
```

The rule of the Trainium skill that was weighed there ("TensorE: Matmul & The Clock Gate", Part 3, a weight load overlaps matmuls in flight only where the row group differs) gave 14.4 more. That rule is about weight loads; that the matmuls of a pair would then go one after another was the prediction's own step, and it did not hold. The weight loads of this batch take 0.68 of its 3.54, so they could be no large part of it. What counts is that the two matmuls run side by side, and the kernel with both in one place shows what they cost if not.

**E** was -4.5 for -3.4. PE's bracket ahead of the transposes is 1.11 for 1.2 forecast, and 3.11 before [rows 10]. The transposes themselves run in 3.68 for 5.29, which the forecast did not have, and what stands behind them gave 0.9 for 1.5:

```profile
4589.68 3.68 PE L3717 MATMUL ps<-ident,x 128*128 128x128 f32 x32 [1.11 <-PEq L3155]
```

**The rival of steps held up by POOL** was right in kind: 2.28 for a COPY of 8 columns above. It takes at most one step of a decode, and the kernel before had it too (2.05 and 2.38).

**What stays open.** The unchanged mixers differ between kernels, 456.8 to 467.7 in layer 0 and 270.6 to 277.3 in layer 1. Of the 42 that the forecast was off, 5.8 lie there. Why they differ was not tried, and neither was why DVE's stand for rows of u costs PE more in the changed kernel than in the others.

## What to carry to other kernels

Where a planner deals one engine's work out to another's units, and that engine is full, its partner can be no further than the work dealt ahead of it allows. So a step made cheaper must be read through the plan: lower costs put more steps ahead of the same unit, and the saving is gone. Keep the old costs, or carry what a unit overspends, and add up the full engine's measured time ahead of a unit before counting a wait as gone. A step moved to an idle engine was not free here: a neighbour's step beside it took over twice its time. Compare the neighbour's step with and without it.

## What was not expected of the hardware

- Two 32-bit matmuls of 512 columns whose results go to partitions 0 to 7 and 32 to 39 run side by side: 0.89 for the pair; with all of them added up in one place, 0.87 each.
- A two-input step on DVE (128x1024, 1.22) beside a subtraction on POOL (2.4) took up to 3.1, and steps of 0.17 to 0.29 took 2.1 to 2.5 when they met one. The Trainium skill, "SBUF — State Buffer", Who interferes with whom, says that the two engines hold a shared pair of ports for a whole instruction; these rows agree, for the COPY of 2.28 above ends at 957.0, as does POOL's subtraction that began at 954.65.
